# Indirect row transfers of an expert layer: four sizes chosen by branches, or always 128 rows

## The chip, the cores and the metric

The kernel runs on one core of one Trainium2 chip. The metric is the device time of one execution in microseconds (us); lower is better. The kernel is written directly against the engines: TensorE (PE), VectorE (DVE), ScalarE (ACT), GpSimd (POOL) and SyncE (SP), each with its own instruction stream, kept in step by semaphores.

## The reference

One layer of a decoder trunk is computed for 1024 new prompt tokens and 64 sample tokens, 1088 in all: RMSNorm, one input projection, four token mixers, one output projection, residual; then RMSNorm, a mixture of experts and a residual; then a final RMSNorm. The change touches the mixture of experts only. Cut to it, the reference is:

```python
lg = xt @ rg_w + rg_b                       # 4 groups, top 1
le = (xt @ re_w + re_b).reshape(n, 4, 8)    # 8 experts in each, top 2 of the chosen group
gates = ...                                 # (n, 32), two entries per token are not zero
hg = einsum('nd,edf->nef', xt, w_gate)      # 32 experts, d = 1024, f = 128
hu = einsum('nd,edf->nef', xt, w_up)
act = silu(hg) * hu * gates[:, :, None]
out = einsum('nef,efd->nd', act, w_down)
```

Every token goes to two experts, so there are 2176 (token, expert) pairs. How they fall on the experts follows from the inputs. Worked out from the reference's own routing, the 32 experts get, in order, 76 38 59 38 63 79 60 13 34 74 42 11 14 23 37 13 134 90 97 119 88 127 52 111 110 69 36 44 81 135 135 74 pairs.

## The kernel before, in words

The first part (projection, mixers, output projection, router) ends at about 380 us of the span. The router builds an integer table: for expert e, column `tab[:, 9e]` holds the pair numbers of its first 128 pairs in rows 0, 1, 2, ..., and the value 2^20 in every row beyond them; `gidxs` is the same shifted right by one, the token's row (2^19 where there is none). Pairs over 128 form overflow blocks, here three, of 6, 7 and 7 pairs. So there are 35 blocks.

A block passes through these steps:

1. POOL gathers its token rows (4 KB each) from `scratch_h` in HBM into one of four buffers `xg` with an indirect DMA (line 1137). An index above `bounds_check` moves no row.
2. PE transposes the rows (line 2194); ACT (line 906) and DVE (line 1663) copy them out, split into a high and a low part.
3. The weights (gate, up, down; 512 KB each) are loaded by SP (line 532) into one of eight buffers (`wfirst` for three, `wlater` for five). The load for block b is issued when the down product of block b-8 is done (line 539). ACT (`at_whi`, line 922) and DVE (line 1679) split gate and up; ACT's copy waits until all three parts have landed.
4. PE multiplies (lines 2216 to 2218), ACT and DVE form the activation, PE transposes it (line 2227) and multiplies by the down matrix (line 2239).
5. ACT and DVE copy the result into one of two buffers `outb` (lines 946 and 1654), after the scatter of two blocks before has landed.
6. POOL scatters the rows of `outb` to `scratch_out` in HBM by pair number (line 1152), once both halves are there.

PE's products do not depend on how many rows are live: each block is computed as 128 rows. POOL's stream in steady state alternates: gather of block b+4, scatter of block b-1, gather of b+5, scatter of b, and so on. A gather waits for the transposes of the block that had its buffer, a scatter for the two output copies. All weights go through the queue of SP, all gathers and scatters through the queue of POOL; both queues are served by the same 16 DMA engines.

After the last scatter has landed, POOL writes `gcol` (line 1194), which lets SP load the pairs back (line 593), nine tiles; the two rows of each token are summed with its residual, normalised and stored.

The size of a transfer is chosen at run time in `by_size`: the index column's rows 64 and then 96 (or 32) are read into a register and compared, so a block of n pairs is issued with 32, 64, 96 or 128 rows. Of the 35 blocks 8 are issued with 32 rows, 11 with 64, 8 with 96 and 8 with 128. The first three gathers are issued with 128 rows whatever they hold.

Of the kernel before, what the change touches and what calls it, by code (L numbers as in the profile page):

```python
# [27 lines left out]
P = 128  # L28
# [11 lines left out]
NE, NG, EG, FF = 32, 4, 8, 128  # L40
# [3 lines left out]
Q = P // 4  # L44
NONE = 1 << 20
# [73 lines left out]
def build_layer(nc, a):  # L119
    with ExitStack() as ctx:  # L120
# [19 lines left out]
        def at(name, shape, offset, dt=F32):  # L140
            return nc.alloc_sbuf_tensor_at("at_" + name, shape, dt, offset=lo + offset)
# [51 lines left out]
        gcol = at("gcol", [P, OVER], o_sg + 3904, I32)  # L193
        scol = at("scol", [P, OVER], o_sg + 3968, I32)
# [29 lines left out]
        tab = at("tab", [P, TCOLS], o_uc + 8192 + TCOLS * 4, I32)  # L224
        gidxs = at("gidxs", [P, TCOLS], o_uc + 8192, I32)
# [191 lines left out]
        def mf_wait(eng, name):  # L417

            n = M_AT[name]
            eng.wait_ge(s["mf_" + M_USES[n][1]], nth([u for _, u in M_USES], n))  # L420
# [182 lines left out]
        def _(act):  # L603
# [95 lines left out]
            def conv_state_part(c):  # L699

                name = f"cst{c}"
                b = ps[:, m_bank(name), :]
                m_out(name, [stage[0:n, m, c * P:(c + 1) * P] for m, (n, _, _) in enumerate(c_outs)],
                      [b[0:n, q:q + P] for n, q, _ in c_outs])
                if c == 1:
                    for m, (n, _, dst) in enumerate(c_outs):
                        act.dma_start(dst, stage[0:n, m, :]).then_inc(s["stage_out"], 16)
                        stages[0] += 16
# [333 lines left out]
        def _(pool):  # L1042
# [69 lines left out]

            last_token, last_pair = pool.to_reg(NT - 1), pool.to_reg(2 * NT - 1)

            def by_size(pairs, move):


                def has(r):
                    return pool.value_load(pairs[r:r + 1, :], min_val=0, max_val=NONE) < NONE

                with pool.If(has(2 * Q)):
                    with pool.If(has(3 * Q)):
                        move(4 * Q)
                    with pool.Else():
                        move(3 * Q)
                with pool.Else():
                    with pool.If(has(Q)):
                        move(2 * Q)
                    with pool.Else():
                        move(Q)  # L1130

            def gather(b, index, pairs, free=None):

                def move(n):
                    if free is not None:
                        pool.wait_ge(s["xt_done"], free)
                    g.indirect_dma_start(xg[0:n, b % XG, :], None, hs,  # L1137
                                         bass.IndirectOffsetOnAxis(ap=index[0:n, :], axis=0),
                                         bounds_check=last_token, oob_is_err=False)\
                        .then_inc(gath[b % XG], 16)  # L1140

                if b < 3:
                    move(P)
                else:
                    by_size(pairs, move)

            def scatter(b, index):

                def move(n):
                    pool.wait_ge(s["ob_act"], b + 1)  # L1150
                    pool.wait_ge(s["ob_dve"], b + 1)
                    g.indirect_dma_start(orow, bass.IndirectOffsetOnAxis(ap=index[0:n, :], axis=0),  # L1152
                                         outb[0:n, b % 2, :], None, bounds_check=last_pair,
                                         oob_is_err=False).then_inc(scat[b % 2], 16)

                by_size(index, move)


            pool.wait_ge(s["xg_zero"], XG)
# [3 lines left out]
            def gather_over(o):  # L1163

                with pool.If(total > o):
                    col = pool.value_load(ovt[0:1, OVER + o:OVER + o + 1], min_val=0,
                                          max_val=TCOLS - 1)

                    do(g.tensor_copy(gcol[:, o:o + 1], gidxs[:, bass.ds(col, 1)]), s["gcol_ready"])
                    do(g.tensor_copy(scol[:, o:o + 1], tab[:, bass.ds(col, 1)]), s["scol_ready"])  # L1170
                    gather(NE + o, gcol[:, o:o + 1], scol[:, o:o + 1], NE + o - 3)

            for b in range(-XG, NE + 1):
                n = b + XG
                if n == 3:
                    pool.wait_ge(s["idx_ready"], 2)
                if n < NE:
                    c = n * CAPB
                    gather(n, gidxs[:, c:c + 1], tab[:, c:c + 1], b + 1 if b >= 0 else None)
                else:  # L1180
                    if n == NE:
                        pool.wait_ge(s["ov_ready"], 1)
                        total = pool.value_load(ovt[0:1, 2 * OVER:2 * OVER + 1], min_val=0,
                                                max_val=OVER)
                    gather_over(n - NE)
                if b >= 1:
                    c = (b - 1) * CAPB
                    scatter(b - 1, tab[:, c:c + 1])
# [7 lines left out]
            def over_from(o):  # L1196

                if o == OVER:
                    return
                with pool.If(total > o):  # L1200
                    if o + XG + 1 < OVER:
                        gather_over(o + XG + 1)
                    scatter(NE + o, scol[:, o:o + 1])
                    with pool.If(total < o + 2):
                        all_scattered(NE + o + 1)
                    over_from(o + 1)
# [1140 lines left out]
```

## Time and profile before

| | us |
|---|---|
| median of three runs | 628.34 |
| the three runs | 628.34, 629.05, 624.61 |
| the profiled execution | 627.64 |
| its span, first to last instruction | 625.6 |

| engine | busy us | share of the span |
|---|---|---|
| PE | 591.6 | 95% |
| DVE | 474.2 | 76% |
| ACT | 283.4 | 45% |
| POOL | 106.8 | 17% |

The profile is one execution. 2.0 us of it lie outside the span. The expert part runs from about 380 to 589 us, the final part from there to the end. The page divides the span into 40 slices; it gives for each engine the busy share, for the DMA engines the mean busy share of all 16 and the rate. Queue q1 is SP's, queue q0 POOL's. A "packet" is one transfer record of one DMA engine.

### The profile page before, as it was taken

How to read it: one execution, taken by the hardware profiler on the slowest of the kernel's cores; microseconds unless marked ns; L12 is line 12 of the kernel's file. 1: busy time of each engine (PE TensorE's matmuls, PEld its weight loads, DVE VectorE, ACT ScalarE, POOL GpSimd, SP SyncE). 2: the span in 40 equal slices, each digit the busy share in tenths (PEclk: the TensorE clock that was granted, in tenths of full speed). 3: DMA queues.
4: the chain of work that ended last, by engine and by line, in shares of the span. 5: the costliest groups of instructions: out<-in, count | busy, mean ns of one | idle time of the engine just before them, and what ended most of it. 6: DMA issues, size and time to landing. Idle time of an engine off the chain costs nothing.

```text
span 625.6 us, 10616 instructions
## 1 busy us (share of the span) xinstructions
PE 591.6 (95%) x3539; PEld 503.3 (80%) x3539; DVE 474.2 (76%) x742; ACT 283.4 (45%) x439; POOL 106.8 (17%) x151
## 2 busy tenths in 40 slices
PE   8899999999999999999999977999999999999776
PEld 6799999997998898788888756888888888778322
DVE  4938997999999687465566587898887878587177
ACT  6642112230313336222221145777777777576434
POOL 4300001000000000000000004133344444333100
PEclk9999999999999999999999987999999999999899
DMA  8750210221113203654112147999999999972399
GB/s 305 149 148 7 67 35 4 65 56 35 35 42 125 77 3 121 192 201 169 67 69 102 50 146 252 335 381 362 355 348 371 376 379 344 370 297 108 74 422 370
DMA packets 53511, 115.98 MB, mean 185 GB/s; under 512 B 10627, under 2 KB 28936, under 8 KB 52361
## 3 DMA queue, kind: packets, MB, share of 16 engines
q1 hardware_dynamic: 46069, 96.90, 44.4%
q0 software_dynamic: 6784, 17.84, 8.1%
q8 instruction: 28, 0.46, 0.3%
q10 hardware_dynamic: 596, 0.50, 0.3%
q14 instruction: 34, 0.28, 0.1%
HBM read 99.90 MB, written 20.68 MB: 193 GB/s over the span
## 4 chain that ended last, share of the span: by engine, by line
PE 51%; DVE 14%; DMA 7%; SPq 4%; issue 2%; ACT 2%; POOLq 0%; POOL 0%; DVEq 0%; ACTq 0%
PE ps L2091 13%; PE ps L1913 8%; PE ps L2239 7%; DMA at_wlater<-in_expert_w_down 4%; PE ps L2217 4%; PE ps L2216 4%; PE ps L2218 4%; SPq L532 4%; PE ps L2194 3%; DMA at_opair_p<-scratch_out 2%; DVE at_mixP L1284 2%; PE ps L2155 2%; PE ps L2313 2%; DVE at_hT L1243 1%; DVE at_lnsq L1470 1%
## 5 line engine op out<-in xcount | busy, mean ns | idle before, releaser
L1913 PE MATMUL ps<-at_hT,at_ring 128*128 128x384 f32 x936 | 165.5, 333 | 0.0
L1913 PEld LDWEIGHTS ps<-at_hT,at_ring 128*128 128x128 f32 x936 | 155.9, 188 | 5.1 <-issue 5.0
L2091 PE MATMUL ps<-at_hT,at_mring 128*128 128x512 f32 (+1 forms) x432 | 102.6, 393 | 1.9 <-DVE at_mring L1438 1.2
L2091 PEld LDWEIGHTS ps<-at_hT,at_mring 128*128 128x128 f32 (+1 forms) x432 | 77.3, 182 | 21.1 <-DVE at_mring L1438 1.6
L2216 PE MATMUL ps<-at_whi,at_hTm 128*128 128x256 f32 x280 | 81.0, 289 | 0.0
L1284 DVE SCALAR_TENSOR_TENSOR at_mixP<-at_uc,sb_par,at_mixP 128x1024 f32<-128x1024 f32 x60 | 77.3, 1289 | 2.1
L2218 PE MATMUL ps<-at_whi,at_hTm_lo 128*128 128x256 f32 x280 | 78.2, 279 | 0.0
L1679 DVE TENSOR_TENSOR at_wlater_lo<-at_wlater,at_whi 128x1024 fp32r<-128x1024 f32 x40 | 49.0, 1224 | 14.0 <-ACT at_whi L922 12.6
L1663 DVE TENSOR_TENSOR at_hTm_lo<-ps,at_hTm 128x1024 fp32r<-128x1024 f32 x34 | 41.6, 1224 | 17.1 <-ACT at_hTm L906 16.9
L2216 PEld LDWEIGHTS ps<-at_whi,at_hTm 128*128 128x128 f32 x280 | 52.8, 188 | 0.2 <-issue 0.2
L2218 PEld LDWEIGHTS ps<-at_whi,at_hTm_lo 128*128 128x128 f32 x280 | 52.5, 188 | 0.0
L2194 PEld LDWEIGHTS ps<-sb_ident,at_xg 128*128 128x128 f32 x280 | 36.1, 189 | 17.9 <-issue 17.1
L1137 POOL DMA_INDIRECT at_xg<-scratch_h,at_gidxs x32 | 42.0, 1311 | 42.5 <-issue 31.9
L922 ACT ACTIVATE at_whi<-at_wlater 128x1024 fp32r<-128x1024 f32 x40 | 42.2, 1054 | 14.2 <-DMA at_wlater<-in_expert_w_down 7.2
L2217 PE MATMUL ps<-at_wlater_lo,at_hTm 128*128 128x256 f32 x160 | 44.9, 281 | 0.0
L1152 POOL DMA_INDIRECT scratch_out<-at_outb,at_tab x32 | 30.7, 960 | 74.2 <-DVE at_outb L1654 72.2
L1679 DVE TENSOR_TENSOR at_wfirst_lo<-at_wfirst,at_whi 128x1024 fp32r<-128x1024 f32 x30 | 36.7, 1224 | 6.7 <-ACT at_whi L922 5.7
L906 ACT ACTIVATE at_hTm<-ps 128x1024 fp32r<-128x1024 f32 x34 | 34.9, 1027 | 8.8 <-PE ps L2194 8.8
L2194 PE MATMUL ps<-sb_ident,at_xg 128*128 128x128 f32 x280 | 36.7, 274 | 2.2 <-DMA at_xg<-scratch_h,at_gidxs 2.2
L610 ACT ACTIVATE at_wk<-at_x 128x1024 f32<-128x1024 f32 (+1 forms) x13 | 13.8, 1058 | 53.6 <-DVE at_x L1510 44.7
L2239 PE MATMUL ps<-at_wlater,at_actT 128*128 128x512 f32 x80 | 37.6, 592 | 0.0
L922 ACT ACTIVATE at_whi<-at_wfirst 128x1024 fp32r<-128x1024 f32 x30 | 31.7, 1056 | 5.5 <-PE ps L2218 5.2
(274 smaller groups left out, 904.2 us busy)
## 6 DMA issues: line engine op xcount, KB each, us to landing
at_wlater<-in_expert_w_gate SPq DMA_DIRECT2D x20, 512.0 KB, 8.2
at_wlater<-in_expert_w_up SPq DMA_DIRECT2D x20, 512.0 KB, 10.8
at_wlater<-in_expert_w_down SPq DMA_DIRECT2D x20, 512.0 KB, 17.2
at_raw<-in_w_in SPq DMA_DIRECT2D x16, 512.0 KB, 4.0
at_opair_p<-scratch_out SPq DMA_DIRECT2D x8, 1024.0 KB, 14.6
at_wfirst<-in_expert_w_gate SPq DMA_DIRECT2D x15, 512.0 KB, 6.4
at_wfirst<-in_expert_w_up SPq DMA_DIRECT2D x15, 512.0 KB, 9.5
at_wfirst<-in_expert_w_down SPq DMA_DIRECT2D x15, 512.0 KB, 16.7
```

Source lines behind the costliest of these rows:

```text
L922: nc.scalar.activation(whi[h][:], half(wexp(j), h), ACT.Copy).then_inc(s[f"w_hi{h}"], 1)
L1137: g.indirect_dma_start(xg[0:n, b % XG, :], None, hs, bass.IndirectOffsetOnAxis(ap=index[0:n, :], axis=0), bounds_check=last_token, oob_is_ ...
L1284: do(stt(y, x, par[:, c, k:k + 1], y, ALU.mult, ALU.add))
L1663: v.tensor_tensor(hTm_lo[j % 2][:], src, hTm[:, j % 2, :, :].bitcast(F32), ALU.subtract).then_inc(s["htm_lo"], 1)
L1679: v.tensor_tensor(half(wexp_lo(j), h), half(wexp(j), h), whi[h][:].bitcast(F32), ALU.subtract).then_inc(s[f"w_lo{h}"], 1)
L1913: mm = pe.matmul(ps[:, bank + r, 0:t1 - t0], w[:, wpart, k * P:(k + 1) * P], hT[:, hpart, k, t0:t1], start=(m, wpart, hpart) == (0, 0, 0), ...
L2091: mm = pe.matmul(ps[0:n, b + r, :], mring[:, 1 - i % 2, mpart, k * P:k * P + n], wo[:, wpart, k, r * 512:(r + 1) * 512], start=(c, mpart, ...
L2194: mm = pe.transpose(rows_psum(b)[:, k // 4, k % 4 * P:(k % 4 + 1) * P], xg[:, j % XG, :].rearrange("p (q k) -> p k q", k=KC)[:, k, :], ide ...
L2216: pe.matmul(out, x, high, start=k == 0, stop=False)
L2217: pe.matmul(out, x, low, start=False, stop=False)
L2218: mm = pe.matmul(out, x_low, high, start=False, stop=k == KC - 1)
L2239: mm = pe.matmul(ps[:, bank + r, :], actT[:, j % 2, :], wexp(j)[:, q:q + 512], start=True, stop=True)
```

## The change

`by_size` is removed. Every gather and every scatter is issued with 128 rows, without reading the index column and without a branch. Rows whose index is out of bounds still move no data. Indices, buffers, waits and the order of transfers stay as they are.

```diff
-            def by_size(pairs, move):
...
-                def has(r):
-                    return pool.value_load(pairs[r:r + 1, :], min_val=0, max_val=NONE) < NONE
-
-                with pool.If(has(2 * Q)):
-                    with pool.If(has(3 * Q)):
-                        move(4 * Q)
-                    with pool.Else():
-                        move(3 * Q)
-                with pool.Else():
-                    with pool.If(has(Q)):
-                        move(2 * Q)
-                    with pool.Else():
-                        move(Q)
-
-            def gather(b, index, pairs, free=None):
+            def gather(b, index, free=None):
...
-                if b < 3:
-                    move(P)
-                else:
-                    by_size(pairs, move)
+                move(P)
...
-                by_size(index, move)
+                move(P)
...
-                    gather(NE + o, gcol[:, o:o + 1], scol[:, o:o + 1], NE + o - 3)
+                    gather(NE + o, gcol[:, o:o + 1], NE + o - 3)
...
-                    gather(n, gidxs[:, c:c + 1], tab[:, c:c + 1], b + 1 if b >= 0 else None)
+                    gather(n, gidxs[:, c:c + 1], b + 1 if b >= 0 else None)
```

On POOL, the scatter of block 0 stands so before the change (the list is the program's text, so all four variants stand there, and one of them is executed; `at_tab` is the index column, line 1119 the load of an index into a register):

```order
L1119 TENSOR_LOAD at_tab
L1119 ISA x2
L1121 COMPARE_AND_BRANCH
L1119 TENSOR_LOAD at_tab
L1119 ISA x2
L1122 COMPARE_AND_BRANCH
L1152 DMA scratch_out<-at_outb,at_tab 2176x1024
L1122 UNCONDITIONAL_BRANCH
L1152 DMA scratch_out<-at_outb,at_tab 2176x1024
L1124 UNCONDITIONAL_BRANCH
```

And so after it, from the last instruction of the router on (line 1120 is the gather, line 1132 the scatter):

```order
L1055 TENSOR_TENSOR sb_rs<-sb_ss,sb_mhalf 64x1
L1120 DMA at_xg<-scratch_h,at_gidxs 128x1024 x6
L1132 DMA scratch_out<-at_outb,at_tab 2176x1024
L1120 DMA at_xg<-scratch_h,at_gidxs 128x1024
L1132 DMA scratch_out<-at_outb,at_tab 2176x1024
```

Nothing but the transfers is left on POOL there: two loads, their two register instructions each and two branches are gone ahead of every transfer but the first three gathers. The other engines' streams are unchanged.

## Rows read from the trace of the kernel before

**Rows 1.** The page: the span in 40 slices of 15.6 us; last row over the whole span.

```profile
PE   8899999999999999999999977999999999999776
DMA  8750210221113203654112147999999999972399
GB/s 305 149 148 7 67 35 4 65 56 35 35 42 125 77 3 121 192 201 169 67 69 102 50 146 252 335 381 362 355 348 371 376 379 344 370 297 108 74 422 370
```

**Rows 2.** Core 0 in one stretch: busy us per engine, granted clock, DMA share of 16 engines, GB/s.

```profile
384.40:547.00 162.60, 159.94 (x1076) 132.78 (x1077) 129.75 (x152) 115.12 (x170) 64.15 (x58) 1.00 1.01 359
```

**Rows 3.** ACT in order of time: start, us, instruction, [idle before <-releaser].

```profile
531.78 1.06 ACT L922 ACTIVATE at_whi<-at_wlater 128x1024 fp32r<-128x1024 f32 x1 [0.62 <-DMA at_wlater<-in_expert_w_down]
534.72 0.60 ACT L946 ACTIVATE at_outb<-ps 128x512 f32<-128x512 f32 x1 [0.60 <-DMA scratch_out<-at_outb,at_tab]
539.86 1.06 ACT L922 ACTIVATE at_whi<-at_wlater 128x1024 fp32r<-128x1024 f32 x1 [3.18 <-DMA at_wlater<-in_expert_w_down]
547.01 1.06 ACT L922 ACTIVATE at_whi<-at_wlater 128x1024 fp32r<-128x1024 f32 x1 [3.42 <-DMA at_wlater<-in_expert_w_down]
```

**Rows 4.** DMA queues over 384.4 to 547.0 us: queue, packets, MB, share of 16 engines.

```profile
DMA packets 17388, 58.41 MB, mean 359 GB/s; under 512 B 3165, under 2 KB 3165, under 8 KB 17368
q0 software_dynamic: 5597, 15.30, 26.7%
```

**Rows 5.** DMA issues of 496 to 533 us: KB each, median us from issue to landing.

```profile
at_wlater<-in_expert_w_gate SPq DMA_DIRECT2D x5, 512.0 KB, 9.6
at_wlater<-in_expert_w_down SPq DMA_DIRECT2D x4, 512.0 KB, 25.8
```

**Rows 6.** The chain that ended last, in order of time: start us, us, what.

```profile
468.24 0.88 PE ps L2194 x8
...
520.72 26.27 DMA at_wlater<-in_expert_w_down
```

**Rows 7.** The page: the queue of the gathers and scatters, whole execution.

```profile
q0 software_dynamic: 6784, 17.84, 8.1%
```

**Rows 8.** By stretch, as [rows 2]: the first two gathers, 76 and then 38 live rows.

```profile
382.80:383.40 0.60, 0.20 (x2) 0.01 (x1) 0.57 (x1) 0.60 (x1) 0.30 (x1) 1.00 0.56 225
383.50:384.00 0.50, 0.00 (x0) 0.00 (x0) 0.50 (x1) 0.15 (x1) 0.50 (x1) 1.00 0.44 107
```

**Rows 9.** DMA of 586.3 to 588.7 us, in which the last scatter moved.

```profile
DMA packets 49, 0.05 MB, mean 19 GB/s; under 512 B 41, under 2 KB 41, under 8 KB 48
q0 software_dynamic: 48, 0.03, 5.8%
```

**Rows 10.** Line 1119: duration ns min/median/max, first and last start.

```profile
L1119 POOLq TENSOR_LOAD <-at_tab x122: 283/464/1090, 380.6 to 569.2; - x122
L1119 POOLq TENSOR_LOAD <-at_scol x12: 297/472/690, 546.7 to 584.4; - x12
```

**Rows 11.** POOL in order of time: the first gather, one middle block, the last two scatters.

```profile
379.87 1.30 POOL L1137 DMA_INDIRECT at_xg<-scratch_h,at_gidxs  x1 [9.83 <-DVE at_gidxs L1635]
...
453.94 0.92 POOL L1152 DMA_INDIRECT scratch_out<-at_outb,at_tab  x1 [2.13 <-DVE at_outb L1654]
455.96 1.48 POOL L1137 DMA_INDIRECT at_xg<-scratch_h,at_gidxs  x1 [1.11 <-issue]
...
583.35 0.86 POOL L1152 DMA_INDIRECT scratch_out<-at_outb,at_scol  x1 [3.56 <-DVE at_outb L1654]
586.25 0.86 POOL L1152 DMA_INDIRECT scratch_out<-at_outb,at_scol  x1 [2.04 <-issue]
```

**Rows 12.** DVE in order of time: the right halves of the last two output blocks.

```profile
581.88 0.69 DVE L1654 COPY at_outb<-ps 128x512 f32<-128x512 f32 x1 [1.45 <-PE ps L2239]
583.60 0.69 DVE L1654 COPY at_outb<-ps 128x512 f32<-128x512 f32 x1 [1.02 <-PE ps L2239]
```

**Rows 13.** Landing of the gathers.

```profile
DMA to landing us min/median/max: 4.6/7.7/11.4
```

**Rows 14.** Landing of all transfers of scratch_out.

```profile
DMA to landing us min/median/max: 2.4/6.9/21.6
```

## Prediction, made before the changed kernel ran

> **What bounds the kernel now.** I read the slices of the page first. In the expert part PE and the DMA engines are both full [rows 1]: from 384.4 to 547.0 us PE is busy 159.94 of 162.60 us at full clock, and the 16 DMA engines have a busy share of 1.01 at 359 GB/s [rows 2]. Of the engines' time there 26.7% goes to POOL's queue, the rest to the weights [rows 4]. A block takes PE about 5.6 us: from the scatter of block 10 to that of block 33 are 129.4 us [rows 11], 23 blocks, the waits below among them. The order of time on ACT then shows that the tie is lost to the DMA: the split of the weights waits for `w_down` 0.62, 3.18 and 3.42 us at 531.8, 539.9 and 547.0 us [rows 3], 7.2 us in all, and the chain that ended last goes through the load issued at 520.72, which took 26.27 us to land [rows 6]. That is the load of block 29 (issued behind the down product of block 21).
>
> What is late is not the DMA as a whole but its slowest engine. Gate, up and down loads of one block are issued together, and each gives every engine the same 8 packets of 4 KB; they share one semaphore, so I read the landings of gate, up and down as the 16th, 32nd and 48th of its 48 counts. In 496 to 533 us the 16th comes 9.6 us after issue, the 48th 25.8 us after it [rows 5]. Sixteen evenly loaded engines would finish the second and third transfer 16 packets behind the first, some 3 us. So single engines are more than 10 us behind the others, and every block waits for the last.
>
> **Who loads one engine more than another.** The weights do not, the indirect transfers do. First, a row without an index is a packet too: the last scatter (7 live rows, issued as 32) shows 48 packets of q0, 41 of them tiny [rows 9]: 25 dead rows and 16 semaphore counts. The whole queue confirms it: rows issued are 2912 in gathers and 2752 in scatters, 5664, plus 70 x 16 counts = 6784, the page's number, and 17.84 MB is the 2 x 2176 live rows of 4 KB [rows 7]. Second, the live rows of a 128-row transfer do not spread over all engines. While the second gather (38 live of 128) moved, the share was 0.44, with 76 live it was 0.56 [rows 8]. Each engine has 8 of 128 rows. Neighbouring eights would give 38 rows to 5 engines (0.31), an even deal to 16. What fits is fours: rows 0-3 and 32-35 to the first engine, 4-7 and 36-39 to the next, rows from 64 on to the other eight engines: 38 rows on 8 engines (0.50), 76 on 11, then 8 when the short ones are done (0.69, 0.50).
>
> The Trainium skill, "DMA: Bandwidth & Descriptors", section The descriptor swizzle, gives just that formula for a 128-partition transfer; no row here shows single engines.
>
> **The change, part by part.**
>
> *Spread.* A full engine carries s/16 live rows of an s-row transfer: 2, 4, 6 or 8 for 32, 64, 96 and 128. With 128 always, the first engine carries 8 wherever a block has 36 pairs or more, 6 for the block of 34, 4 for the smaller ones. Counted over what must pass before the load of block 29 can land (gathers 3 to 31, scatters 0 to 25): before 152 + 130 = 282 rows on the first engine, after 210 + 186 = 396. That is 114 more; the total is unchanged.
>
> *The price of one.* In the same 162.6 us the first engine moved 25 loads (5 to 29) x 24 = 600 weight packets plus those 282, so 882, 0.184 us each if it was never idle, and the pace of all engines says the same: 359 GB/s / 16 is 4096 B in 0.183 us. Alone an engine is faster: the whole queue's 8.1% x 16 x 625.6 = 811 us over 4352 rows bounds a live row at 0.186 from above [rows 7]. The 114 rows cost 114 x 0.184 = 21.0 us at today's pace. As other engines run dry the common pace relaxes a little, so I take 0.17: **+19.4 us**. From below: were the common rate the only limit, the cost would be 0.
>
> Nothing covers it: the 8-deep weight prefetch is the cover, and [rows 3] show that it is used up in the before kernel. The new waits will be of the same kind, only earlier: the first at about block 17 to 20 (490 us) instead of 26. PE, ACT and DVE then stand still together, and SP's next loads start later, but the late engine still has its queue full.
>
> *Dead rows.* 8960 instead of 5664 rows, so 3296 more tiny packets. From [rows 9]: 5.8% x 16 x 2.4 us = 2.2 us less 7 live rows of 0.16 or more leaves at most 0.027 us each; below, nothing. The first engine gets 70 x 8 = 560 rows in all, of which 2 x (26 x 8 + 6 + 8 x 4) = 492 are live, so 68 dead ones: 0 to 1.8 us, taken with 0.5. On an average engine 206 x 0.027 = 5.6 us at the very most, on engines that have time.
>
> *POOL's reads.* 134 index loads of 0.46 us median go [rows 10]. In the middle they are hidden: POOL waits 2.1 us for `outb` before each scatter, and the idle 1.1 us ahead of a gather [rows 11] only brings a gather forward whose rows land 7.7 us later [rows 13] and are wanted 12.3 us later (block 16: issued 455.96 [rows 11], transposed at 468.24 [rows 6]). The transfer itself takes POOL no longer with more rows: 1.30 us for 128, 0.86 for 32, both hidden. At the end they show: block 34's output is ready at 583.60 + 0.69 = 584.29 [rows 12], its scatter starts at 586.25 [rows 11]; the scatter before started 583.35 - (581.88 + 0.69) = 0.78 us after its copy. So 586.25 - 585.07 = **-1.2 us**. The last scatter then has 4 rows on one engine instead of 2, **+0.4**.
>
> Sum: 627.64 + 19.4 + 0.5 - 1.2 + 0.4 = 646.5, stated as **646 us**. The profiled execution lies 0.7 us under the median, within the spread of the runs.
>
> **Rivals.**
>
> A. *Common rate, not one engine.* The bytes are the same, so if the 16 engines together were limited by the memory, an engine with more rows would simply be served faster while others idle. An engine alone may reach 0.159 us a packet (412 GB/s over 16; the best slices of [rows 1] have 422). First engine: 996 packets x 0.159 = 158 us, inside the 162.6. Then nothing is added and 627.6 - 1.2 + 0.4 + 0 to 5.6 for dead rows = **627 to 632**. For it: share 1.01 on all. Against it: the 16 us between the 16th and the 48th count. 10%.
>
> The Trainium skill, same page, section Anatomy of one DMA, has a transfer cost 2.0 us plus bytes / 436 GB/s. By that rule the change costs nothing at all, since it moves the same bytes; here a gather took 4.6 us at the least [rows 13].
>
> B. *Not slower: the reads were the cost.* Gathers come 1.1 us earlier per block. This decides only if PE waits for rows; the chain's waits are for weights. Worth 1.2 us at the end and, if the 7.2 us of waits shrank by the earlier gathers leaving the queue, up to 8: **619 to 626**. 4%.
>
> C. *Half way.* The pace relaxes to about 0.17 for all of the late engine's packets: 996 x 0.17 = 169.3, +6.7 over 162.6: **634**, and up to 639. 14%.
>
> D. *The scatter becomes a wait as well.* `outb` has two buffers, so a scatter has two blocks, 11 us, less the 2 us to its issue. Median landing is 6.9 us [rows 14], and one copy already waited 0.60 us [rows 3]. With 8 rows behind a longer backlog, 2 us over for ten blocks is +20 at worst, but a block then takes 6.5 us and the limit moves along: **656 to 665**. 8%.
>
> The forecast itself, 639 to 656: 64%.
>
> **How the numbers follow.** The measurement can tell about 1% (6.3 us). The range takes the forecast, most of C, and leaves A, B and D out but for their edges: 633 to 657. Slower by over 1% (above 634.6): the forecast, D and most of C, 0.84. Within 1%: A, the rest of C and part of B, 0.13. Faster: 0.03.
>
> **What would show it.** Queue q0 must show 8960 + 1120 = 10080 packets with 17.84 MB. If the spread is right, ACT's waits for `w_down` grow from 7.2 to about 27 us and begin near 490 us; the rate over the expert part falls from 359 to about 320 GB/s while the 16th count stays early and the 48th is later than 26 us; the mean DMA share drops under 1. If A holds, the rate stays and the waits too. B would need the waits to shrink, D waits of `at_outb` for `scratch_out` of several us. Wrong would be above all the price per row: it is read from a state in which all engines are busy. Or the rows of a 64- or 32-row transfer are dealt less evenly than s/16, which would make the difference smaller.

## The result, and the profile after

The changed kernel takes 629.32 us (median of 20 runs, 627.64 to 631.5), the kernel before beside it 625.48 us (20 runs, 624.61 to 629.28). The ratio is 1.0051, 95% interval 1.0039 to 1.0062: slower by 0.5%, 3.2 us by the ratio (the medians are 3.8 us apart). The 646 us of the prediction and its range from 633 were too high. The profile before, from which the prediction was worked out, is of an execution of 627.64 us, 2.2 us above the median of 20; the profiled execution of the changed kernel took 629.21, so the two profiles differ by only 1.6 us. Among all executions below, one (of e12) took 1509 us, with PE's products of 128x384 at 702 ns where e1 has 344; it is left out of every ratio, and nothing here explains it.

The page of the changed kernel, its span, the slices and POOL's queue:

```profile
span 627.2 us, 10032 instructions
PE   8899999999999999999999967999999998899775
DMA  8760210211113204644122157999999999982398
GB/s 310 143 144 11 68 34 8 60 56 35 35 42 134 70 1 135 195 184 168 68 91 77 50 165 263 374 340 328 346 364 355 359 371 336 395 298 112 78 421 364
q0 software_dynamic: 10080, 17.85, 7.7%
```

10080 packets and 17.85 MB, as counted: 3296 dead rows more and not a live one. Against [rows 1] the rate in the middle is lower.

Busy time by stretch, same columns as [rows 2], [rows 8]:

```profile
384.40:547.00 162.60, 157.76 (x1061) 130.84 (x1062) 127.72 (x152) 113.81 (x170) 56.32 (x55) 1.00 0.97 355
383.50:384.00 0.50, 0.00 (x0) 0.00 (x0) 0.47 (x2) 0.00 (x0) 0.50 (x1) 1.00 0.37 82
```

PE is busy 157.76 us where it was 159.94, the rate is 355 and no longer 359 GB/s, and the DMA share has fallen under 1, to 0.97: some engines are now idle at times.

ACT in order of time, the waits for weights ([rows 3]):

```profile
510.55 1.06 ACT L922 ACTIVATE at_whi<-at_wlater 128x1024 fp32r<-128x1024 f32 x1 [1.35 <-issue]
...
517.54 1.06 ACT L922 ACTIVATE at_whi<-at_wfirst 128x1024 fp32r<-128x1024 f32 x1 [2.81 <-issue]
...
523.79 1.06 ACT L922 ACTIVATE at_whi<-at_wfirst 128x1024 fp32r<-128x1024 f32 x1 [2.52 <-issue]
...
529.11 1.06 ACT L922 ACTIVATE at_whi<-at_wfirst 128x1024 fp32r<-128x1024 f32 x1 [1.59 <-DMA at_wfirst<-in_expert_w_down]
...
535.55 1.06 ACT L922 ACTIVATE at_whi<-at_wlater 128x1024 fp32r<-128x1024 f32 x1 [2.17 <-DMA at_wlater<-in_expert_w_down]
...
542.69 1.06 ACT L922 ACTIVATE at_whi<-at_wlater 128x1024 fp32r<-128x1024 f32 x1 [3.41 <-DMA at_wlater<-in_expert_w_down]
...
548.60 1.06 ACT L922 ACTIVATE at_whi<-at_wlater 128x1024 fp32r<-128x1024 f32 x1 [2.18 <-issue]
...
553.94 1.06 ACT L922 ACTIVATE at_whi<-at_wlater 128x1024 fp32r<-128x1024 f32 x1 [1.58 <-DMA at_wlater<-in_expert_w_down]
...
558.95 1.06 ACT L922 ACTIVATE at_whi<-at_wlater 128x1024 fp32r<-128x1024 f32 x1 [0.55 <-DMA at_wlater<-in_expert_w_down]
...
565.37 1.06 ACT L922 ACTIVATE at_whi<-at_wfirst 128x1024 fp32r<-128x1024 f32 x1 [1.44 <-DMA at_wfirst<-in_expert_w_down]
```

The six that name `w_down` sum to 10.7 us, 12.6 us in seven waits by the view of all waits, against 7.2 in three. Four more, 1.35, 2.81, 2.52 and 2.18 us (8.9), stand at the same line in the same train with "issue", no releaser that the profile could name; the second profile of this kernel, under e5 below, names them from 514.88 (block 24) on and sums to 16.5 us. I read the four as waits for the same weights, so 12.6 us at least and 21.5 at most. The wait before 542.69 is for block 28, that before 510.55 for block 23. For block 28 it ended at 539.86 before, so these weights are 2.8 us late; those of block 29 are at 548.60 against 547.01, 1.6 us late, as much as the two profiled executions differ. One landing is not the loss: in the second profile of the changed kernel block 28 is only 0.3 us late (540.14) and block 30 is 2.6 us later than before (554.16 against 551.52, where nothing was waited for).

The full engines hold up SP too. An instruction of SP that issues a part of the weights takes 0.33 to 0.43 us when nothing is in its way; from 384 to 545 us 18 of 84 take over 1 us in the kernel before and 44 of 84 in the changed one, up to 5.55 us. The chain that ended last goes through them to the weights of block 28:

```profile
499.56 5.22 SPq L532
...
512.85 2.08 SPq L532
...
516.91 25.76 DMA at_wlater<-in_expert_w_down
542.69 1.07 ACT at_whi L922
```

In e1 below, with the rows dealt evenly, 2 of 88 take over 1 us.

POOL, one middle block, and the end ([rows 11]), and DVE's last copy ([rows 12]):

```profile
454.03 1.01 POOL L1132 DMA_INDIRECT scratch_out<-at_outb,at_tab  x1 [3.23 <-DVE at_outb L1634]
455.34 1.02 POOL L1120 DMA_INDIRECT at_xg<-scratch_h,at_gidxs  x1 [0.31 <-issue]
...
585.34 0.97 POOL L1132 DMA_INDIRECT scratch_out<-at_outb,at_scol  x1 [3.46 <-DVE at_outb L1634]
587.06 0.97 POOL L1132 DMA_INDIRECT scratch_out<-at_outb,at_scol  x1 [0.74 <-DVE at_outb L1634]
590.30 0.10 POOL L1174 MEMSET at_gcol<- 128x1 int32 x1 [2.27 <-DMA scratch_out<-at_outb,at_scol]
```

```profile
585.61 0.69 DVE L1634 COPY at_outb<-ps 128x512 f32<-128x512 f32 x1 [1.03 <-PE ps L2219]
```

The idle time ahead of a gather is 0.31 instead of 1.11 us, the last scatter starts 0.76 us after its output is ready instead of 1.96. But the end does not follow: from the last copy's end (586.30) to POOL's last `memset` are 4.0 us, before 4.4. The two last scatters now run back to back and the last needs 3.2 us to land instead of 2.4.

### The profile page after: what moved, and what is told of

The parts are those of the page before. It is cut to its first block, busy times and chain, and to the rows that moved or that the text cites. A ratio compares the mean times of both kernels' runs of the same rounds, so it can differ in the third digit from the quotient of the medians.

```text
span 627.2 us, 10032 instructions
## 1 busy us (share of the span) xinstructions
PE 592.6 (94%) x3539; PEld 503.1 (80%) x3539; DVE 472.7 (75%) x742; ACT 281.5 (45%) x439; POOL 102.5 (16%) x151
## 3 DMA queue, kind: packets, MB, share of 16 engines
q0 software_dynamic: 10080, 17.85, 7.7%
## 4 chain that ended last, share of the span: by engine, by line
PE 46%; DVE 14%; SPq 9%; DMA 8%; ACT 2%; issue 2%; POOL 0%; DVEq 0%; POOLq 0%; ACTq 0%
PE ps L2071 13%; PE ps L1893 8%; SPq L532 8%; PE ps L2219 5%; DMA at_wlater<-in_expert_w_down 4%; PE ps L2196 3%; PE ps L2197 3%; PE ps L2198 3%; PE ps L2174 3%; DVE at_mixP L1264 2%; DMA at_opair_p<-scratch_out 2%; PE ps L2135 2%; PE ps L2293 2%; DVE at_hT L1223 1%; DVE at_lnsq L1450 1%
## 5 line engine op out<-in xcount | busy, mean ns | idle before, releaser
L1643 DVE TENSOR_TENSOR at_hTm_lo<-ps,at_hTm 128x1024 fp32r<-128x1024 f32 x34 | 41.5, 1221 | 12.6 <-ACT at_hTm L906 12.3
L1132 POOL DMA_INDIRECT scratch_out<-at_outb,at_tab x32 | 32.2, 1007 | 111.2 <-DVE at_outb L1634 110.3
L1120 POOL DMA_INDIRECT at_xg<-scratch_h,at_gidxs x32 | 33.8, 1058 | 19.5 <-DVE at_gidxs L1615 9.8
## 6 DMA issues: line engine op xcount, KB each, us to landing
at_opair_p<-scratch_out SPq DMA_DIRECT2D x8, 1024.0 KB, 14.3
```

The lines of the kernel that those rows point to most:

```text
L1643: v.tensor_tensor(hTm_lo[j % 2][:], src, hTm[:, j % 2, :, :].bitcast(F32), ALU.subtract).then_inc(s["htm_lo"], 1)
```

## The experiments

Each was timed beside the kernel before on the same chip; ratios are to that. Four measures are worked out from the traces of all of them.

The first is the time of a live row in POOL's queue over 401 to 478 us: share x 16 engines x 77 us, less 0.009 us for every packet that is not a live row, over the live rows (MB / 4096 B). (0.009 is what e9 below gives, and 9 ns is the median of the small packets in the trace.) The second is the count of packets that the fullest engine must move before the weights of block 28 can land, by the pattern of fours (for transfers of fewer than 128 rows, s/16 as in the prediction); the third is the time from 384.4 us to that landing over the count. It takes the fullest engine as never idle. The fourth is the share of weight packets (4 KB, SP's queue, 401 to 533 us) that took at most 161 ns.

| kernel | ratio, 95% interval | us per live row | packets before block 28 | landed at | us per packet | weight packets of at most 161 ns |
|---|---|---|---|---|---|---|
| before | 1 | 0.184 | 576 + 146 + 124 = 846 | 539.9 | 0.184 | 58% |
| changed | 1.0051 [1.0039, 1.0062] | 0.169 | 576 + 202 + 178 = 956 | 542.7 | 0.166 | 91% |
| e5 changed again | 1.0046 [1.0025, 1.0068] | 0.171 | 956 | 540.1 | 0.163 | 92% |
| e1 dealt | 0.9938 [0.9919, 0.9957] | 0.161 | about 815 | in time | | 86% |
| e2 eights | 1.0159 [1.0137, 1.0182] | 0.173 | 576 + 224 + 200 = 1000 | 548.6 | 0.164 | 91% |
| e3 reads kept | 1.0068 [1.0041, 1.0094] | 0.166 | 956 | 543.2 | 0.166 | 91% |
| e6 fixed sizes | 0.9963 [0.995, 0.9977] | 0.180 | 846 | in time | | 57% |
| e7 gathers 128 | 0.9975 [0.9957, 0.9992] | 0.161 | 576 + 202 + 124 = 902 | in time | | 93% |
| e8 scatters 128 | 1.0088 [1.0067, 1.0109] | 0.195 | 576 + 146 + 178 = 900 | 544.9 | 0.178 | 59% |
| e10 mirrored | 1.0039 [1.0012, 1.0065] | 0.169 | 956 | 542.5 | 0.165 | 92% |
| e11 gathers 96 | 1.0021 [1.0006, 1.0036] | 0.177 | 576 + 184 + 124 = 884 | 539.2 | 0.175 | 62% |

The share tells the two forms apart sharply, the mean much less. Over 384.4 to 547.0 us the mean 4 KB packet of all 16 engines and both queues took 182 ns before, 184 in e8, 180 in e11, 175 in the changed kernel, 171 in e7 and 168 in e1: where most weight packets are short, a few are very long (over 300 ns: 4% in the changed kernel, 2% before).

### e1, e2 and e10: the same rows, dealt otherwise

Theory 1 was that the fullest DMA engine sets the landing of the weights and the price per packet is lower than I took. Theory 2 that only the common rate counts. The three kernels change nothing but the partition that a rank gets:

```diff
+        rowid = wsT[:].rearrange("p h i -> p (h i)")[:, TCOLS:TCOLS + P]
...
+            do(g.iota(rowid, [[8, 2], [64, 2], [1, 8], [16, 4]], base=0, channel_multiplier=0, **flt))   # e1
+            do(g.iota(rowid, [[64, 2], [4, 2], [8, 8], [1, 4]], base=0, channel_multiplier=0, **flt))    # e2
+            do(g.iota(rowid, [[-64, 2], [1, 64]], base=64, channel_multiplier=0, **flt))                 # e10
...
-                    do(ts(prow[q, k, :], cols[q, 0:P], row[q, k:k + 1], None, ALU.is_equal))
+                    do(ts(prow[q, k, :], rowid[q, 0:P], row[q, k:k + 1], None, ALU.is_equal))
```

> The changed kernel (128 rows always, nothing read), with one thing different: the router's table gives rank r of an expert to another partition, so that every 16 consecutive live rows go to 16 different DMA engines if the pattern of fours read from the first gathers holds. Same rows, same bytes, same dead rows. Theory 1 (uneven engines cost, at a relaxed price): the most loaded engine carries about 286 live rows instead of 492, the waits for w_down (about 12 us in the changed kernel, 7.2 before) go, 617 to 621 us. Theory 2 (only the common rate limits): as the changed kernel, 629 us. If the pattern of fours is not how the rows are dealt, a time anywhere above.

Measured 622.91 us, 0.9938, a little short of the 617 to 621 us that theory 1 gave; run once more with e11:

> The dealt kernel of e1 again, beside e11, for its interval: 622 to 624 us, 0.992 to 0.996 of the kernel before.

623.2 us, 0.9948 [0.9928, 0.9968]. e1, by stretch, and its landings as in [rows 5]:

```profile
384.40:547.00 162.60, 162.25 (x1098) 135.08 (x1098) 133.62 (x157) 119.77 (x177) 60.84 (x60) 1.00 1.01 384
```

```profile
at_wlater<-in_expert_w_gate SPq DMA_DIRECT2D x5, 512.0 KB, 5.8
at_wlater<-in_expert_w_down SPq DMA_DIRECT2D x5, 512.0 KB, 9.7
```

PE is busy 162.25 of 162.60 us, at 384 GB/s. No wait for weights is left. The 48th count comes 9.7 us after issue instead of 25.8: the late engines are gone. This kernel beats both others, by 0.6% the one before and, over the two ratios, by about 1.1% the changed one.

> The changed kernel with the rows dealt as badly as possible: each 8 consecutive ranks go to one DMA engine, so the first engine carries 556 live rows instead of 492 (440 instead of 396 before the load of block 29). Theory 1, with a packet of 0.165 us on an engine that runs nearly alone: 44 x 0.165 = +7 us, 635 to 638 us. With the price of the prediction, 0.184: +8. Theory 2: 629 us.

Measured 637.21 us, 1.0159, inside the expectation of theory 1. ACT's waits for weights, and the one for block 28:

```profile
ACT at_whi L923 <- DMA at_wlater<-in_expert_w_down: 21.5, 10, 3.4
ACT at_whi L923 <- DMA at_wfirst<-in_expert_w_down: 19.0, 8, 3.3
```

```profile
472.99 1.06 ACT L923 ACTIVATE at_whi<-at_wfirst 128x1024 fp32r<-128x1024 f32 x1 [1.25 <-DMA at_wfirst<-in_expert_w_down]
...
548.57 1.06 ACT L923 ACTIVATE at_whi<-at_wlater 128x1024 fp32r<-128x1024 f32 x1 [2.28 <-DMA at_wlater<-in_expert_w_down]
```

They sum to 40.5 us and begin at 473 us. Same bytes, same dead rows, same form, 14 us between e1 and e2: the load of the fullest engine is the cause, and theory 2 falls.

> The changed kernel with ranks 0 to 63 of every expert in partitions 64 to 127 and ranks 64 to 127 in 0 to 63: the same uneven load, laid on the other eight DMA engines. If the loss is the load of the fullest engine, whichever it is: as the changed kernel, 1.003 to 1.007. If there are slower engines among the first or the last eight, it moves by more.

Measured 629.78 us, 1.0039. It does not matter which eight engines are the full ones.

### e7, e8 and e11: which direction changes the price

```diff
 # e7, in gather
-                if b < 3:
-                    move(P)
-                else:
-                    by_size(pairs, move)
+                move(P)
```

```diff
 # e8, in scatter
-                by_size(index, move)
+                move(P)
```

> Only the gathers are issued with 128 rows, the scatters keep their sizes: 210 instead of 152 rows on the first engine before block 29's weights, 58 of the 114 more. If both halves of the change cost and gain alike: 1.002 to 1.004. The share of weight packets that take 159 ns (about 57% before, about 90% after) tells which direction slows them: if gathers of 32 to 96 rows, which write to SBUF, do it, the share goes to 90% here and stays at 57% in the run with scatters only.

> Only the scatters are issued with 128 rows: 186 instead of 130 rows on the first engine, 56 of the 114. If both halves are alike 1.002 to 1.004; if the price of a packet falls only with the gathers, this one pays 56 x 0.18 = 10 us less what the other engines' idle time gives back, so 1.005 to 1.015.

Measured 624.67 us, 0.9975, and 631.87 us, 1.0088: opposite signs, so the two halves are not alike. POOL's queue over 401 to 478 us, first the kernel before, then e7, e8 and the changed kernel:

```profile
q0 software_dynamic: 2265, 5.52, 20.8%
```

```profile
q0 software_dynamic: 3097, 5.65, 19.3%
```

```profile
q0 software_dynamic: 3051, 5.17, 21.3%
```

```profile
q0 software_dynamic: 3996, 5.55, 20.5%
```

e7 moves more live rows (5.65 against 5.52 MB) and more dead ones in less engine time (19.3 against 20.8%). The row falls from 0.184 to 0.161 us. In e8 it does not fall. So beside the weights the gathers of 32 to 96 rows made packets long, the scatters did not. The weights' own packets say it as well: 58% took at most 161 ns before, 59% in e8, 93% in e7 and 91% in the changed kernel.

A scatter in a small form does have long packets where no weights move beside it. The 74 rows of block 31's scatter, with no packet of the weights in the stretch, took 220 ns on average in the 96-row form (before; 217 in e7) and 165 in the 128-row form (e8). The last scatter's seven rows took 198 to 308 ns in the 32-row form (before), 159 to 164 in the 128-row form (changed kernel).

e11 keeps fixed sizes and needs no reads for the gathers, but in the 96-row form:

```diff
+FULL = [16, 18, 19, 21, 23, 24, 29, 30]
...
-                if b < 3:
-                    move(P)
-                else:
-                    by_size(pairs, move)
+                move(P if b < 3 or b in FULL else 3 * Q)
```

> Gathers of 96 rows for every block of at most 96 pairs (128 for the rest), with no reads ahead of them; scatters as before. Against e7 (all gathers 128) the dead rows are nearly as many, 21 of the 29 gathers that count have another form. If it is the form of 32 to 96 rows that makes packets long, a live row of POOL's queue costs 0.18 us again, the first engine's load is 600 + 190 + 130 = 920 packets x 0.184 = 169 us, +7 over before's 162: 1.005 to 1.012, with waits for w_down of 15 us and more. If any fixed size that needs no reads is good: as e7, 0.996 to 0.999.

Measured 627.81 us, 1.0021, under the range that I had set, with 7.1 us of waits for `w_down`, not 15. Its queue:

```profile
q0 software_dynamic: 2751, 5.65, 20.8%
```

Against e7 it has fewer packets on the fullest engine (884, 902) and is slower, its row costs 0.177 instead of 0.161, and 62% of the weight packets take at most 161 ns, not 93%. So it is the form, not dead rows; and not the reads, since e6 below, without them, has 57% and 0.180, and e3, with them, 91% and 0.166.

### e3 and e6: the reads

e3 makes all four branches of `by_size` issue 128 rows; e6 writes each block's size into the program:

```diff
 # e3, in by_size, and so for move(2 * Q) and move(Q)
-                        move(3 * Q)
+                        move(4 * Q)
```

```diff
 # e6, SIZES is the list of the sizes that by_size picks
-                if b < 3:
-                    move(P)
-                else:
-                    by_size(pairs, move)
+                move(P if b < 3 else SIZES[b] * Q)
...
-                by_size(index, move)
+                move(SIZES[b] * Q)
```

> The kernel before with all four branches issuing 128 rows: the index reads and branches stay, the rows are those of the changed kernel. Against the changed kernel (629.3) it tells what the reads cost: 1.2 us at the end if nothing else shows, so 630.5; up to 4 us more if POOL's reads for the overflow blocks showed too. A rival has the reads hidden: 629.

> The kernel before with each block's size (32, 64, 96 or 128 rows) written into the program instead of read: the same transfers, no reads, no branches. It isolates the reads. If they cost what the end of the chain shows: 1.2 us less than before, 0.998. If they hid more (the overflow blocks' reads, 2.6 us ahead of three gathers): up to 3 us less. If nothing: 1.000.

e3: 631.57 us, 1.0068 [1.0041, 1.0094]. e6: 623.87 us, 0.9963 [0.995, 0.9977]. Without the reads the sized transfers are 2.3 us faster; with them the 128-row ones are about 0.2% slower, an amount inside the intervals of both. The end of e6:

```profile
579.67 0.86 POOL L1150 DMA_INDIRECT scratch_out<-at_outb,at_scol  x1 [3.55 <-DVE at_outb L1652]
581.39 0.86 POOL L1150 DMA_INDIRECT scratch_out<-at_outb,at_scol  x1 [0.85 <-DVE at_outb L1652]
585.30 0.10 POOL L1192 MEMSET at_gcol<- 128x1 int32 x1 [3.05 <-DMA scratch_out<-at_outb,at_scol]
```

```profile
579.93 0.69 DVE L1652 COPY at_outb<-ps 128x512 f32<-128x512 f32 x1 [1.03 <-PE ps L2237]
```

From the last copy's end (580.62) to the `memset` are 4.7 us, not less than the 4.4 before. The end has gained nothing, then; the gain lies in the waits for weights, of which e6's profile shows none. How the reads feed them is not settled: part of it may be that the profile of before was one of the longer executions (627.64, median 625.48).

### e4 and e9: dead rows alone

```diff
 # e4, ahead of the scatter of every block; e9 issues it behind the scatter, with rows of 4 bytes, and waits only at the end
+                    if b >= 2:
+                        pool.wait_ge(s["dead_in"], 16 * (b - 1))
+                    g.indirect_dma_start(dead[:], None, a["router_group_w"][0],
+                                         bass.IndirectOffsetOnAxis(ap=deadi[:], axis=0),
+                                         bounds_check=last_dead, oob_is_err=False)\
+                        .then_inc(s["dead_in"], 16)
```

> The kernel before plus one indirect transfer of 128 dead rows (16 bytes each, no index in range) per block, 32 in all: 4096 more dead packets spread evenly, more than the 3296 of the change, no live row moved elsewhere. Theory 1 (dead rows cost next to nothing, under 0.01 us each on an engine): 256 x 0.009 = 2.3 us of each engine's time at most, 0 to +2.5 us, 625.5 to 628. The rival that the change's loss is the dead rows alone: +3 us or more, 628.5 and up. One transfer more on POOL takes 1 us of its 2 to 3 us of idle time.

Measured 656.55 us, 1.0481, far off. The waits of e4:

```profile
ACT at_outb L948 <- DMA scratch_out<-at_outb,at_tab: 71.8, 26, 4.3
POOL sb_dead L1193 <- DMA sb_dead<-in_router_group_w,sb_deadi: 34.3, 23, 2.9
```

```profile
402.21 1.27 POOL L1193 DMA_INDIRECT sb_dead<-in_router_group_w,sb_deadi  x1 [0.30 <-issue]
403.98 0.94 POOL L1154 DMA_INDIRECT scratch_out<-at_outb,at_tab  x1 [0.50 <-issue]
...
408.99 1.25 POOL L1193 DMA_INDIRECT sb_dead<-in_router_group_w,sb_deadi  x1 [1.57 <-DMA sb_dead<-in_router_group_w,sb_deadi]
411.22 0.92 POOL L1154 DMA_INDIRECT scratch_out<-at_outb,at_tab  x1 [0.98 <-issue]
```

My wait did it, not the rows: a transfer that moves no byte, issued at 402.21, has landed only at 408.99. POOL stood for it, the scatters came late, and ACT waited 71.8 us for `outb`. e4 says nothing on the price of a dead row.

> The kernel before plus one indirect transfer of 128 dead rows per block, as in e4, but issued behind the scatter and waited for by nobody until the end (in e4 POOL waited for the one before and came late with its scatters). 4096 dead packets more, spread evenly. At 0.009 us each they are 2.3 us of each engine's time, of which an engine that is never idle shows all: 0 to +2.5 us, 1.000 to 1.004. If dead rows were the loss of the change: 1.005 or more.

Measured 628.83 us, 1.0035 [1.0007, 1.0063]: 2.2 us (0.4 to 3.9 by the interval) for 4096 dead rows on 16 engines, 0.009 us each; the median small packet in the trace takes 9 ns too. The 3296 of the change would be 1.8 us if they fell evenly. They don't: 68 of them are on the first engine by the count of the prediction, 0.6 us, and the rest mostly on engines that have time.

### e5: the changed kernel again

> The changed kernel once more, beside the three below: 629 to 630 us, 1.004 to 1.006 of the kernel before.

629.7 us, 1.0046 [1.0025, 1.0068]. Its waits for weights:

```profile
ACT at_whi L922 <- DMA at_wlater<-in_expert_w_down: 10.5, 5, 3.2
ACT at_whi L922 <- DMA at_wfirst<-in_expert_w_down: 6.0, 3, 3.3
```

From e6 to e5, both without reads, are 5.2 us by the ratios (5.8 by the medians) on the same chip: that is what the 128-row form costs by itself.

## Why the prediction was wrong

**What bounds the kernel: right.** The slowest DMA engine sets the landing of the weights. e1 takes its load away and the waits with it.

**The spread: right.** Fours, eight engines first. e1, e2 and e10 order themselves by the count of the fullest engine. The packet records of the last scatter, seven live rows with nothing beside them, show the pattern itself: in the changed kernel its rows start in pairs, at 588.60, 588.76 and 588.92 us, and one at 589.07, so two engines have four and three of them; in e2 they start one by one, 0.155 us apart, in e1 all within 0.06 us. (The share while the second gather moved, 0.37 here and 0.44 before, is read from 0.5 us and is the weaker sign.)

**The price of one: the step that failed.** I wrote: "The 114 rows cost 114 x 0.184 = 21.0 us at today's pace. As other engines run dry the common pace relaxes a little, so I take 0.17". I took this for the price of the additional rows only and left the other 882 packets at 0.184. The change moves the price of all: with gathers of 128 rows a packet of the fullest engine costs 0.165 us. Up to the load of block 29, the prediction's own mark, 996 packets took 164.2 us (548.60 less 384.4) where 882 took 162.6: the 114 at the old price are 21.0 us more, and 0.0195 us less on each of 996 gives 19.4 back. What is left is 1.6 us, the difference of the two profiled executions. The same 0.163 to 0.166 stands in e2, e3, e5 and e10; 0.178 and 0.175 stand in e8 and e11, in which most gathers are of 32 to 96 rows.

I had the reason for the fall wrong too, in the main. My case C, "Half way", has the pace relax because other engines run dry, and takes 0.17 for all packets. In e8, with a full engine of 900 packets and the gathers as before, the price falls from 0.184 to 0.178: that may be this relaxing, and it is about a third of the fall. The rest, to 0.166, comes only with the gathers of 128 rows, and in e7 the row costs 0.161 though the share is 0.99. That a transfer's form could slow the others was not among my rivals. The 0.186 us of [rows 7] that I took as a sign that an engine alone is faster shows nothing of the kind; it lies above 0.184.

**Rival A** gave 627 to 632 us, which holds the time, for a reason that the runs refute: it had the waits stay as they were, and they grew from 7.2 to 12.6 us or more and began at block 23 or 24. That its range holds the time is luck: a fuller engine and cheaper packets nearly cancel, and e1 and e2, with the same bytes, lie 14 us apart.

**Dead rows: right.** 0.5 us taken for the first engine; e9's price and its 68 dead rows give 0.6.

**The reads: wrong place.** I took 1.2 us at the end; there it is 0.4 at most, since two scatters back to back land later. In all they are worth 2.3 us (e6).

**Sum by the runs:** -2.3 (reads), +0.6 (dead rows), +4.6 (rest of the 5.2 between e6 and e5: fuller engine less cheaper packets) = +2.9, beside +3.2 in the result. This is no independent check: -2.3 and 5.2 are both taken from the ratios of e5 and e6, so they give e5's ratio back. The sum of the prediction itself comes to 646.7, not 646.5.

**The waits.** Forecast were 27 us from block 17 to 20 on; they came from block 23 or 24 on, as fits the smaller price, with 12.6 to 21.5 us. I had set their growth equal to the loss, and that was wrong too: the loss is how much later the last block that waits gets its weights. ACT's split runs ahead of PE, so a part of each wait costs nothing. Against e1 (no waits, 622.9) the 7.2 us of the kernel before go with 3.9 us more on the same chip (2.3 of them fall away with the reads, by e6), the 40.5 us of e2 with 14.3: a third to a half of the waiting is seen at the end. The 0 and 7.2 us of waits of e6 and the kernel before, 2.3 us apart, fit that.

## What to carry to other kernels

Where DMA is full, count packets per engine, not bytes: a row transfer with dead rows behind live ones fills half the engines and every other transfer waits for them. Keep the 128-row form, whose packets were the shortest here, and deal the live rows over the partitions so that each engine gets its share; an iota with another pattern did it at no cost. When a change alters the form of a transfer, price all packets anew, those of other queues too.

## What the runs showed of the hardware

- Beside the weights, gathers of 32 to 96 rows made packets of both queues longer, to 0.184 us a row against 0.161; scatters of these sizes did not (e7, e8, e11), but alone they have long packets of their own, 220 ns against 165 (block 31's scatter). Why was not tried. The Trainium skill, "SBUF — State Buffer", section Door 1: The DMA port swizzle, puts partitions 0-3 with 32-35 on one port and 64-67 with 96-99 on another; an engine that takes four neighbouring partitions of a 64-row gather would then share a port with another engine. Engines that share a port would fit the 220 ns, and they would fit that gathers, which write to SBUF as the weight loads do, disturb these and scatters, which read, don't; that is a reading, and no run here shows ports.
- A transfer of 128 dead rows took 6.8 us to land between full queues (e4), a dead row 0.009 us of an engine (e9).
- Live rows at the front of a 128-row transfer sit on few engines: seven of them on two (changed kernel), on one or on seven when dealt otherwise (e2, e1).
- With full queues the instruction that issues a load takes SP up to 5.55 us instead of 0.33 to 0.43 (changed kernel).
- The page's HBM line counts dead rows as if they had moved, while the queue's MB does not:

```profile
HBM read 99.90 MB, written 20.68 MB: 193 GB/s over the span
```

```profile
HBM read 106.32 MB, written 27.76 MB: 214 GB/s over the span
```

6.42 MB more read is 1568 rows of 4 KB, 7.08 MB more written is 1728 rows: the rows added to gathers and scatters, all dead.
